# Grouped attention: values stationary, probabilities streaming, outputs with the features on partitions

## The reference

```python
def attend(qb):
    s = jnp.einsum('bqkgd,bskd->bkgqs', qb, k).astype(jnp.float32) * scale
    p = jax.nn.softmax(s, axis=-1).astype(v.dtype)
    return jnp.einsum('bkgqs,bskd->bqkgd', p, v)

qa, ka, va, za, qb, kb, vb, zb, ga, gb = split_cols(proj)
oa = gqa_attention(qa, ka, va) * jax.nn.silu(za)
ob = neighbourhood_attention(qb, kb, vb, rpb) * jax.nn.silu(zb)
ya = jnp.einsum('ble,ed->bld', oa, w_o_attn)
yb = jnp.einsum('ble,ed->bld', ob, w_o_na)
mixed = jax.nn.sigmoid(ga) * ya + jax.nn.sigmoid(gb) * yb
return x + jnp.einsum('bld,de->ble', mixed, w_out)
```

## Time and profile before

| | us |
|---|---|
| median of 3 runs | 1746.45 (1742.07 to 1750.2) |
| profiled execution | 1755.85 |
| its span, first to last instruction | 1754.5 |
| TensorE busy | 1694.3, 97% of the span |
| VectorE busy | 863.7, 49% |
| ScalarE busy | 612.2, 35% |
| value matmuls (2644), both layers | 3% of the chain that ended last |
| mean granted TensorE clock | 0.969 of full |

### The profile page before, as it was taken

One profiled execution on the slowest core, in us unless ns is written; L12 is line 12 of the kernel. 1 busy time (PEld: TensorE's weight loads), 2 busy tenths in 40 slices (PEclk: granted clock), 3 DMA queues, 4 the chain that ended last, 5 costly groups with the idle time before them and its releaser, 6 DMA issues.

```text
span 1754.5 us, 24500 instructions
## 1 busy us (share of the span) xinstructions
PE 1694.3 (97%) x10253; PEld 1446.4 (82%) x10253; DVE 863.7 (49%) x1552; ACT 612.2 (35%) x1084; POOL 51.9 (3%) x52
## 2 busy tenths in 40 slices
PE   7999989989999999999999999999999999999997
PEld 5897877778888888899888788999988988777886
DVE  3434555656645655854444334347444444334443
ACT  5242244343322335533343332223323233332333
POOL 0000000000000000020000000000110000000000
PEclk9999979999999999999999899999999998899999
DMA  6225200023333322412103001233311202012331
GB/s 187 72 76 114 79 13 13 25 81 111 96 96 96 96 96 79 102 57 65 49 26 84 25 13 61 84 97 119 76 60 49 73 25 73 13 37 72 108 101 55
DMA packets 163118, 125.19 MB, mean 71 GB/s; under 512 B 32176, under 2 KB 159792, under 8 KB 163008
## 3 DMA queue, kind: packets, MB, share of 16 engines
q1 hardware_dynamic: 163008, 123.63, 24.3%
HBM read 121.52 MB, written 2.10 MB: 70 GB/s over the span
## 4 chain that ended last, share of the span: by engine, by line
PE 89%; DVE 3%; ACT 3%; issue 2%; DMA 2%; SPq 1%; POOL 0%; DVEq 0%; ACTq 0%; POOLq 0%
PE bank L570 67%; PE bank L2644 3%; PE bank L2978 2%; PE bank L2621 2%; PE bank L2953 2%; PE bank L2631 2%; PE bank L1575 2%; PE bank L1534 1%; PE bank L2551 1%; PE bank L2965 1%; PE bank L1461 1%; ACT w_hi L517 1%; PE bank L2504 1%; DMA na_bias_a<-na_rel 1%; ACT probs L1514 1%
## 5 line engine op out<-in xcount | busy, mean ns | idle before, releaser
L570 PE MATMUL bank<-h_hi,w_hi 128*128 128x512 f32 (+2 forms) x920 | 330.4, 379 | 9.1 <-issue 5.0
L526 DVE TENSOR_TENSOR w_lo<-w_raw,w_hi 128x2048 fp32r<-128x2048 f32 (+2 forms) x117 | 241.2, 2061 | 184.2 <-ACT w_hi L517 183.9
L570 PE MATMUL bank<-h_lo,w_hi 128*128 128x512 f32 (+2 forms) x920 | 325.2, 373 | 0.0
L570 PE MATMUL bank<-h_hi,w_lo 128*128 128x512 f32 (+2 forms) x920 | 323.9, 372 | 0.0
L517 ACT ACTIVATE w_hi<-w_raw 128x2048 fp32r<-128x2048 f32 (+2 forms) x117 | 201.1, 1719 | 67.3 <-DMA w_raw<-w_in 31.4
L570 PEld LDWEIGHTS bank<-h_hi,w_hi 128*128 128x128 f32 (+1 forms) x920 | 168.5, 191 | 54.9 <-issue 21.6
L570 PE MATMUL bank<-g_hi,w_hi 128*128 128x264 f32 (+1 forms) x784 | 197.7, 315 | 2.4 <-DVE g_lo L1687 2.4
L570 PE MATMUL bank<-g_lo,w_hi 128*128 128x264 f32 (+1 forms) x784 | 194.7, 312 | 0.0
L570 PE MATMUL bank<-g_hi,w_lo 128*128 128x264 f32 (+1 forms) x784 | 194.0, 311 | 0.0
L570 PEld LDWEIGHTS bank<-h_hi,w_lo 128*128 128x128 f32 (+1 forms) x920 | 168.3, 191 | 31.1
L570 PEld LDWEIGHTS bank<-h_lo,w_hi 128*128 128x128 f32 (+1 forms) x920 | 168.1, 191 | 30.1 <-issue 0.5
(11 more groups left out here) (551 smaller groups left out, 2693.9 us busy)
## 6 DMA issues: line engine op xcount, KB each, us to landing
w_raw<-w_in SPq DMA_DIRECT2D x49, 1024.0 KB, 5.3
w_raw<-w_up SPq DMA_DIRECT2D x32, 512.0 KB, 4.9
w_raw<-w_down SPq DMA_DIRECT2D x8, 1024.0 KB, 5.0
w_raw<-w_out SPq DMA_DIRECT2D x8, 1024.0 KB, 5.0
w_raw<-w_in SPq DMA_DIRECT2D x24, 256.0 KB, 4.5
w_raw<-w_out SPq DMA_DIRECT2D x8, 512.0 KB, 3.4
w_raw<-w_ple_gate SPq DMA_DIRECT2D x4, 1024.0 KB, 4.9
w_raw<-w_o_attn SPq DMA_DIRECT2D x8, 512.0 KB, 3.5
```

Of the source, the lines that this page charges most:

```text
L526: DV.e.tensor_tensor(wlo[u % RING][:, 0:n], raw[u % RING][:, 0:n], whi[u % RING][:, 0:n].bitcast(F32), ALU.subtract).then_inc(*w_low(u))
L570: ins = PE.e.matmul(out, stationary[a](k), moving[b](k)[i], start=first and n == 0, stop=last and n == 2)
```

## The change

The value matmuls swap sides: 64 columns of `va` are stationary and 128 columns of turned probabilities stream. Group 0 writes partitions 0 to 63 of bank 6 and group 1 partitions 64 to 127, at columns 128 j for pair j. So the output has its features on partitions, and the 16 transposes of `orow` at the layer's end go. `pe_gated_features` stays for the near attention alone as `pe_near_features`.

A row sum now belongs to a column of the output and can't be applied per partition. So the inverse is written 64 times over per head (`y.wide`, 128x512, by one reciprocal with a repeated source), turned by four transposes into bank 4 (`pe_inverse`), and multiplied in by `dv_normed` after the next tile has begun. Bank 6 is emptied by a plain copy. The meta keys' matmul becomes four of 128 columns. Since bank 4 is used for the inverses, the turn of the third head of a tile waits for `dv_normed`.

The new order of features (pair by pair instead of group by group) needs the gate's weights in pairs of 64 columns, four DMAs instead of one for each of those units, and the rows of `w_o_attn` permuted; the latter is done while the inputs are laid out.

```diff
@@ the plan of the weight units
-            plan_cols(w, C_ZA, C_QB)
+            for a in range(2):
+                plan(w, 0, KT, head_pairs(C_ZA, a))
@@ def pe_tile_out(l, ph, t, qn, first):
             PE.wait_ge(*m_flip.at(l, ph, t))
-            PE.e.matmul(bank[0:qn, 6, 0:NH * AD], y.pmT[t % 2][:, 0:qn], y.v_own[:, :], start=first, stop=True,
-                        skip_group_check=True).then_inc(*product("tile", l, ph, t))
+            if ph == "g":
+                for j in range(4):
+                    ins = PE.e.matmul(bank[:, 6, j * P:(j + 1) * P], y.v_own[:, j * P:(j + 1) * P], y.pmT[t % 2][:, :],
+                                      start=False, stop=True, skip_group_check=True)
...
@@ def dv_tile_out(l, ph, t, qn, first, dst):
-            DV.e.reciprocal(src, src).then_inc(*tile_step(l, ph, t, "inverse"))
+            if ph == "g":
+                if t:
+                    DV.wait_ge(*product.at("inverse", l, t - 1))
+                ins = DV.e.reciprocal(y.wide[:, :].rearrange("p (x d) -> p x d", x=AH), src.unsqueeze(2).broadcast_to([P, AH, AD]))
+            else:
+                ins = DV.e.reciprocal(src, src)
+            ins.then_inc(*tile_step(l, ph, t, "inverse"))
...
-                by_head = src.rearrange("p (j g) -> p g j", g=2)
-                for g in range(2):
-                    cols = slice(g * 4 * AD, (g + 1) * 4 * AD)
-                    ins = DV.e.tensor_tensor(dst[:, cols].rearrange("p (h d) -> p h d", h=4),
-                                             bank[0:qn, 6, cols].rearrange("p (h d) -> p h d", h=4),
-                                             by_head[:, g, :].unsqueeze(2).broadcast_to([qn, 4, AD]), ALU.mult)
+                ins = DV.e.tensor_copy(dst, bank[:, 6, :].rearrange("p (j q) -> p j q", j=4))
@@
+        def pe_inverse(l, t):
+            for j in range(4):
+                PE.wait_ge(*tile_step.at(l, "g", t, "inverse"))
+                ins = PE.e.transpose(bank[:, 4, j * P:(j + 1) * P], layers[l].wide[:, j * P:(j + 1) * P], ident[:, :])
+            ins.then_inc(*product("inverse", l, t))
+
+        def dv_normed(l, t):
+            dst = layers[l].orow[:, :, t * P:(t + 1) * P]
+            DV.wait_ge(*product.at("inverse", l, t))
+            DV.wait_ge(*tile_done(l, "g", t))
+            DV.e.tensor_tensor(dst, dst, bank[:, 4, :].rearrange("p (j q) -> p j q", j=4), ALU.mult).then_inc(*evac_d("normed", l, t))
@@ def pe_gqa(l, fill): turn, value and the end
-                if i > 1:
+                if t and x == 2:
+                    PE.wait_ge(*evac_d.at("normed", l, t - 1))
+                elif i > 1:
                     PE.wait_ge(*g_flip.at(l, i - 2))
...
+                if t and x == 1:
+                    PE.wait_ge(*g_flip.at(l, i - 1))
+                    pe_inverse(l, t - 1)
...
-                    ins = PE.e.matmul(bank[:, 6, h * AD:(h + 1) * AD], y.gpt[i % 3][:, k, :], y.va[:, k, g * AD:(g + 1) * AD],
-                                      start=x == 0 and k == 0, stop=False, skip_group_check=True)
+                    ins = PE.e.matmul(bank[rows, 6, j * P:(j + 1) * P], y.va[:, k, rows], y.gpt[i % 3][:, k, :],
+                                      start=j == 0 and k == 0, stop=False, skip_group_check=True)
...
             next(fill)
+            PE.wait_ge(*g_flip.at(l, AH * TT - 2))
+            pe_inverse(l, TT - 1)
...
-            pe_gated_features(l, "g", lambda k: next(z) if k % 2 else None)
+            for _ in range(2):
+                next(z)
@@ def dv_gqa(l, fill): turn
+                if t and x == 1:
+                    dv_normed(l, t - 1)
@@ def dv_gated_features(l, ph, after):
-                DV.wait_ge(*product.at("of", l, ph, k))
+                DV.wait_ge(*(evac_d.at("normed", l, TT - 1) if ph == "g" else product.at("of", l, ph, k)))
...
-                DV.e.scalar_tensor_tensor(y.z[:, k, 0:S], y.z[:, k, 0:S], 0.5, bank[:, 4 + k % 2, :], ALU.mult,
-                                          ALU.mult).then_inc(*evac_d("of", l, ph, k))
+                DV.e.scalar_tensor_tensor(y.z[:, k, 0:S], y.z[:, k, 0:S], 0.5, y.orow[:, k, :] if ph == "g" else bank[:, 4 + k % 2, :],
+                                          ALU.mult, ALU.mult).then_inc(*evac_d("of", l, ph, k))
```

More of the change, by code:

```diff
@@ L401, in program @@
             y.gpt[2], gpt_end = place(f"gqa_probsT2_{L}", [P, TT, P], F32, c)
+            y.wide, wide_end = place(f"inverse_{L}", [P, NH * AD], F32, gpt_end)
             y.bias, c = place(f"na_bias_{L}", [P, NH, 2 * P], F32, R)
@@ L419, in program @@
             y.M_lo, c = place(f"mixed_lo_{L}", [P, KT, T2], F32R, c)
-            assert c <= sg_at and gpt_end <= sg_at + 3 * 4 * T2
+            assert c <= sg_at and wide_end <= sg_at + 3 * 4 * T2, (wide_end, sg_at + 3 * 4 * T2)
             y.zt = y.sg[:, 3, :]
@@ L2550, in pe_tile_out @@
             PE.wait_ge(*m_flip.at(l, ph, t))
-            PE.e.matmul(bank[0:qn, 6, 0:NH * AD], y.pmT[t % 2][:, 0:qn], y.v_own[:, :], start=first, stop=True,
-                        skip_group_check=True).then_inc(*product("tile", l, ph, t))
+            if ph == "g":
[3 more added lines that the diff above has]
+            else:
+                ins = PE.e.matmul(bank[0:qn, 6, 0:NH * AD], y.pmT[t % 2][:, 0:qn], y.v_own[:, :], start=first, stop=True,
+                                  skip_group_check=True)
+            ins.then_inc(*product("tile", l, ph, t))
         def dv_tile_out(l, ph, t, qn, first, dst):
@@ L2638, in value @@
                 i, (j, g) = AH * t + x, pair_of[x]
-                h = 4 * g + j
+                rows = slice(g * AD, (g + 1) * AD)
                 if x == 0 and t:
@@ L2745, in value @@
                     DV.wait_ge(*g_exp.at(l, AH * t + x))
-                    dv_tile_out(l, "g", t, P, False, y.orow[:, t, :])
+                    dv_tile_out(l, "g", t, P, False, y.orow[:, :, t * P:(t + 1) * P])
             filled(items_g, first_steps(fill, fill_in_gqa(l)), fill_in_gqa(l), score, turn, value)
             next(fill)
+            dv_normed(l, TT - 1)
             if not y.last:
@@ L2781, in pe_meta_queries @@
             PE.wait_ge(*mq_exp.at(l))
+            PE.wait_ge(*evac_d.at("normed", l, TT - 1))
             for k in range(TT):
@@ L2815, in ac_meta_queries @@
                 rows = slice(n * AD, (n + 1) * AD)
-                ins = AC.e.activation(y.omT[rows, :, :].rearrange("p (g jj) m -> p g jj m", g=2),
-                                      bank[rows, 5, 0:P].rearrange("p (g jj n m) -> p n g jj m", g=2, jj=2, n=2)[:, n, :, :, :],
-                                      ACT.Copy)
+                ins = AC.e.activation(y.omT[rows, :, :], bank[rows, 5, rows].rearrange("p (j m) -> p j m", j=4), ACT.Copy)
             ins.then_inc(*om_in(l))
@@ L2838, in dv_meta_queries @@
             next(fill)
-            DV.wait_ge(*g_valued.at(l, n - 2))
+            DV.wait_ge(*g_valued.at(l, n - 1))
             DV.wait_ge(*mq_valued.at(l))
@@ L2853, in flip_before, with pe_near_features @@
                 return evac_d.at("of", l, ph, k - 2)
-            if ph == "n":
-                return a_flip.at(l, 4 * TT - 2 + k)
-            if layers[l].last:
-                return g_flip.at(l, AH * TT - 2 + k)
-            return (mq_flip, om_in)[k].at(l)
-        def pe_gated_features(l, ph, after):
+            return a_flip.at(l, 4 * TT - 2 + k)
+        def pe_near_features(l, after):
             y = layers[l]
             for k in range(4):
-                PE.wait_ge(*flip_before(l, ph, k))
+                PE.wait_ge(*flip_before(l, "n", k))
                 for t in range(TT):
                     ins = PE.e.transpose(bank[:, 4 + k % 2, t * P:(t + 1) * P], y.orow[:, t, k * P:(k + 1) * P], ident[:, :])
-                ins.then_inc(*product("of", l, ph, k))
+                ins.then_inc(*product("of", l, "n", k))
                 after(k)
@@ L2924, in program, with turned_before @@
         items_a = [(t, x) for t in range(TT) for x in range(4)]
+        def turned_before(l, i):
+            if layers[l].last:
+                return g_flip.at(l, AH * TT - 1) if i else evac_d.at("normed", l, TT - 1)
+            return (mq_flip, om_in)[i].at(l)
         def pe_na(l, fill):
@@ L2998, in pe_na @@
             PE.wait_ge(*tile_done(l, "n", TT - 1))
-            pe_gated_features(l, "n", lambda k: next(mix) if k % 2 else None)
+            pe_near_features(l, lambda k: next(mix) if k % 2 else None)
             PE.close(("na", l))
```

8 lines of the change are left out of this document (5 added, 3 removed).

## The result

The changed kernel took 1766.28 us (median of 4 runs, 1765.18 to 1769.22), beside 1748.2 for the kernel before in runs taken with them: 1.012 times as long, 95% interval 1.0089 to 1.015. That is slower, as forecast, but more than was worked out: the ratio makes about 21 us (18.1 by the two medians) where the sum gave 9.1, and 1766.28 lies 10.7 us above the forecast of 1755.6.

The account below looks back on a forecast made before the run. TensorE was taken to bound the grouped attention, with a bias DMA chain behind it. Value matmuls, own-key matmul, inverse transposes and waits summed to +9.1 us, taking the median from 1746.45 to 1755.6 us; range 1743 to 1767.

Parts of the forecast that it names:

- Value matmuls: TensorE's value passes, 64 heads in two layers: 0.89 us per head instead of 0.84, +3.2 us.
- I charge nothing: Value passes in a tile of 64 of the array's columns: changing to that tile and back costs 0.
- Rival 3: Value passes: column tiles cost what row tiles cost, 64 x 0.14 = 9.0 us more, 1764.6 us; chance 0.09.
- the waits in the same sum: TensorE stalls behind reciprocal and copy at tile ends: +1.2 us in layer a, +0.3, +1.1 and +0.4 in b.
- Own-key matmul: Eight times, 2 passes of 512 columns become 8 of 128: 8 x -0.02 = -0.2 us.
- Inverse transposes: Four added per tile on TensorE, 0.44 us, seven of eight groups counted: +3.1 us.
- Reciprocal: VectorE at tile ends, 128x8 becomes 128x512: estimated 2.3 to 3.1 us long, 3.1 taken.
- Removed transposes and DMAs at nothing: 16 transposes fewer per layer, covered by the bias DMA wait, and gate units fetched in four pieces: both worth 0.
- the cover that the prediction relied on: TensorE's work between 946 and 961 us is hidden because the near attention awaits the last bias DMA anyway.
- Rival 5: Granted clock changes: full at the near attention, 1735.0 us, chance 0.05; one more slow grouped-attention stretch, 1762.5 us, chance 0.07.

Follow-up runs that it names:

- the run with 128 columns streaming: Kernel before, each value pass streaming both groups' 128 value columns in place of 64: 1746.62 us, 0.9992 of the kernel before.
- the narrow reciprocal: Changed kernel with a 128x8 reciprocal and a copy spreading it to 128x512, in place of the 128x512 reciprocal: 1763.92 us, 1.0097 of the kernel before.
- interleaved kernel: Changed kernel with the value passes of a pair's two heads alternating between the column halves, key block by key block: 1744.25 us, 0.9974 of the kernel before.
- full-array run: Changed kernel with all 128 value columns stationary and all 128 partitions written in each value pass: 1756.36 us, 1.0048 of the kernel before.
- run with 64 stationary columns: Kernel before with only 64 of 128 columns of turned probabilities stationary in each value pass: 1736.76 us, 0.9924 of the kernel before.

## Why the prediction was wrong

- **Value matmuls: the step that failed.** Predicted +3.2 us. Measured in layer a: 32 x 0.09 for the transposes ahead, and the 32 stretches of values 32.37 us long instead of 27.48: 7.8 us, 15.6 in two layers. The failing sentence is "I charge nothing": the change of column tile was priced by the earlier trace rows, an fp32r projection and a transpose, and the plain f32 case differs from both. Of the 15.6 some 1.8 are the larger pass (the run with 128 columns streaming), against 3.2 predicted; the rest, 13.8, is the change of tile, put at nothing. Rival 3 was the right mechanism, its 0.14 per head too low: it took 0.09 for the entry and 0.05 for leaving, and the traces show 0.14 in and up to 0.19 out. That its 1764.6 lies near the measured time is partly luck, since the waits in the same sum were too high. Its chance of 0.09 was far too small. The Trainium skill ("TensorEngine Tiling (Array Packing)", Key Properties) says that changing the tiling mode drains the engine. The traces agree in that f32 matmuls lose 0.33 us per stay in the changed kernel; transposes of 64 columns lose nothing (0.12 and 0.11 us between starts).
- **Own-key matmul: wrong sign.** Predicted -0.2. Its first pass now comes out of a column tile: 1.09 for 1.00 us, and 0.92 for 0.51 where a projection follows, 4.18 for 3.53 us in layer a, +1.3 in both.
- **Inverse transposes: right.** Four take 0.44 us, and 0.53 where values follow, which is the entry counted above.
- **Reciprocal: right.** 3.35 us for 3.1. The waits at the first two ends of layer a, predicted 0.6 each, are 0.33 ahead of the inverse transposes (838.48 to 839.30 less 0.49) and 0.10 behind them; the turn near 1438 (now at 1453.38) waits 0.74. That is less than the 1.2 + 1.8 predicted; a TensorE that comes later covers more of VectorE's time, which is the likely reason but wasn't tested.
- **Waits that go, not foreseen.** Before, three score pairs in layer b waited 0.59, 0.48 and 0.48 us for an exponential (the earlier trace rows is one); in the changed kernel three wait 0.9 us in all. One wait of 0.25 us for a copied head went too. So layer b lost 9.1 us up to the end of its last unit, layer a 11.3.
- **Removed transposes and DMAs at nothing: right** within the intervals. In the changed kernel's trace the near attention still waits for the bias DMA. Its landing differs by up to 5 us between kernels, with and without these edits; here the stretch from the last unit to the first near turn came out 1.0 us shorter in layer a and 2.4 longer in layer b. Why the landing differs stays open. In executions where it ends the wait no longer, as with the narrow reciprocal, TensorE's own work is the chain there, and the cover that the prediction relied on is gone.
- **Clock.** Rival 5 didn't occur as a cause. But the profiled execution before was one of a low clock, so the two spans understate the change by nearly half (12.2 us for 21.7). The near attention has more idle time before it only in layer b (3.57 us for 0.31); in layer a, where more was forecast too, it fell from 1.86 to 0.87. The DMA still ended the wait there, but two waits of the gate steps for emptied banks (0.54 and 0.87 us) stand where the transposes stood.

With the two terms as measured (3.2 becomes 15.6, -0.2 becomes 1.3) the sum is 23.0 instead of 9.1. With the waits as measured too (0.9 us in layer a; in layer b 0.74 came and 0.65 + 0.25 went; 0.7 in all instead of 3.0) it is 15.6 + 1.3 + 3.1 + 0.7 = 20.7. The two layers lost 20.4 up to the ends of their last units, and what follows up to the first near turns, where the bias DMA ends the wait, makes it 21.7.

## What to carry to other kernels

Price a change of TensorE's tile from rows of the same kind of matmul: a row of another kind or type that shows nothing is no evidence. With 128 columns streaming, the 64-column tiles paid here only where passes of one stood next to passes of the other and both heads were ready, since then two ran in the time of one; alone, each stay cost two edges. Compare profiled spans only after comparing their granted clocks, or by stretches that the change doesn't touch.

## What the runs showed of the hardware

- f32 matmuls in a tile of 64 columns: 0.20 and 0.16 us between starts on entry, 0.20 and 0.21 on leaving, where 0.11 is the pace (changed kernel, 835.11 to 836.54); transposes of that shape 0.12, 0.11 (kernel before, 984.16 to 984.50).
- Passes of both halves, alternating, start in pairs: 16 in 1.03 us (interleaved kernel), where 8 of one half take 1.02 (changed kernel).
- The pace of an f32 pass is 0.11 us with 128 stationary columns and 64 or 128 streaming (kernel before, full-array run), 0.11 with 64 stationary and 128 streaming (changed kernel), and 0.055 to 0.06 with 64 of both (run with 64 stationary columns).
- A VectorE reciprocal of 512 elements per partition takes 3.35 us; with 163 ns for one element that is 6.2 ns for each further one.
